# Second block: both heads of a pair transposed in one run of TensorE, the second into an idle weight-tile bank

## The chip, the cores and the metric

One core of one Trainium2 chip runs the whole program in one launch. The metric is the device time of that launch in microseconds (us).

## What is computed

Two transformer blocks follow each other on 256 tokens of width 2048, in fp32. The first (depth 1) mixes a gated MLP, dilated attention and sparse attention, then cross-attends and runs an MLP. The second has two layers; the change lies in their attention. Each layer projects the normed input to queries, keys and values of three branches with heads of 64 columns, attends, norms each branch, projects back, and runs a squared-relu MLP of width 8192:

```python
for l in range(DEPTH_2):
    h = rmsnorm(x, norm_mix[l])
    proj = jnp.einsum('bsd,de->bse', h, w_in[l])
    ...
    oa = window_attention(qa, ka, va, a_sink[l], t5_table)       # A: 8 heads
    ob = neighborhood_attention(qb, kb, vb, b_rpb[l])            # B: 8 heads
    oc = axial_global_attention(qc, kc, vc, c_q_gain[l], c_k_gain[l])   # C: 16 heads
    mix = jnp.concatenate([rmsnorm(oa, ...), rmsnorm(ob, ...), rmsnorm(oc, ...)], axis=-1)
    x = x + mix @ w_o[l]
    x = x + jnp.square(relu(rmsnorm(x) @ w_up[l])) @ w_down[l]
```

Each attention head is a softmax of scores (256 by 256) times values. The kernel computes scores and probabilities with the queries on partitions, but the product with the values needs the keys there, so each head's probabilities are transposed on TensorE between the two.

## The kernel before

**The stream of units.** Almost all time goes into products with weights. A weight tile of 128 by 1024 arrives by DMA (`wt`), ScalarE rounds it to fp32r (`wh`, step "split"), VectorE forms the rest (`wl`), and TensorE multiplies by both. A unit is two such tiles. In an ordinary unit (`unit`, L371) the result of 16 pairs of matmuls lies in one PSUM bank. In a value unit (`value_unit`, L433) the tokens are on partitions: two banks are open at once and held over several units. An ordinary unit's bank is emptied at the start of the next one: ScalarE takes one half out (`tA`, counted by `a_half`), VectorE adds the other (`tB`, counted by `v_sum`).

**The banks.** PSUM has eight banks, in one tensor `ps`. Banks 0 to 2 are the main banks, which the units take in turn (`next_bank`, L295). Banks 3 and 4 (`bS`) hold the scores of the two heads of a pair, bank 5 (`bP`) takes transposes, bank 6 (`bO`) the attention outputs, bank 7 (`bM`) small sums and norms.

**The planner.** `make_plan` (L142) runs in Python before anything is emitted and writes one list of steps; every engine then emits its instructions in the order of that list, so every engine's queue is fixed. Units are the main line. Attention work is written as generators in a list `tasks`. In every unit, at matmul pair 8 (`n in stages`, in `marks`, L322), `step_bg` (L240) moves each generator on by one step. The instructions of all these steps stand together on TensorE between two halves of a unit; below, this is called a run. Functions in the list `at13` are called at pair 13 of the same unit.

**A pair of heads** (`two_heads`, L1193) goes through: scores of both heads into banks 3 and 4, and the exponentials ("score2"); the division, which leaves the probabilities in a tile `sS` (counted by `v_prob`); the transposes; and the product with the values ("av"), one run later. A head's turn (`turn_head`, L1143; `prob_turn`, L2076) is four transposes of 128 by 128 from `sS` into one bank, then one copy of that bank to a tile `sP`: ScalarE copies the first head (L2393, `a_pcopy`), VectorE the second (L2742, `v_pcopy`). The product of the first head with the values waits for `a_pcopy`, that of the second for `v_pcopy`. The first head is turned in the run at pair 8, the second is put on the list `late` and so is turned at pair 13:

```python
        pts = [sP.grab() for _ in hds]
        turn_head(hds[0], pts[0], 0)
        late.append(lambda: turn_head(hds[1], pts[1], 1))
        yield
```

In branch C, and in the last pairs of B, both heads use bank 5, so the second turn waits for the first head's copy (`a_pcopy`). In A and the first pairs of B the second head uses bank 7 (`apart`).

**Waits.** `give` writes down which semaphore counts make a buffer free, `take` hands them to its next user, and `let_go` (L1708) emits them as waits. There are 16 pairs of heads in each of the two layers (C0 to C7, A0 to A3, B0 to B3), so 32 second turns.

Of the kernel before, what the change touches and what calls it, by code (L numbers as in the profile page):

```python
# [141 lines left out]
def make_plan():  # L142

    p = Plan()
# [90 lines left out]
    deferred, pending, at3, at10, at13, after_unit = [], [], [], [], [], []  # L235
    held = {"evac": False, "s1": 0}

    late = []

    def step_bg():  # L240
        held["s1"] = 0
        for g in list(tasks):
            if next(g[0], "end") == "end":
                tasks.remove(g)
                g[1]["done"] = True
        at13.extend(late)
        late.clear()

# [30 lines left out]
    def run_at13():  # L279
        while at13:  # L280
            at13.pop(0)()
# [8 lines left out]
        else:  # L290
            step("mm", h, k, k + 1)

    banks = {"n": 0, "held": set()}

    def next_bank():  # L295

# [49 lines left out]

    def unit_end():
        run_at13()
        while after_unit:
            after_unit.pop(0)()  # L350

# [19 lines left out]
    def unit(parts, nk, src, thin=False, stages=(8,), ahead=2, early=False, tail=False):  # L371

        u = unit_begin(ahead)
        n = 0
        for j, (first, last, ev) in enumerate(parts):
            if first:
                next_bank()
            g = len(groups) - 1
            for k in range(nk):
                marks(n, None if len(parts) == 1 else max(1, 4 - n // 4) if thin else 0, stages, early)  # L380
                if (thin or tail) and n == 11:
                    run_pending()
                h = where[2 * u + n // 8][1]
                end = last and k == nk - 1
                if thin:
                    half = 2 * k // nk
                    tiles[h].append((g, src(j, k % (nk // 2)), k % (nk // 2) == 0, end, half, (k + 1) % (nk // 2) == 0))
                else:
                    tiles[h].append((g, src(j, k), first and k == 0, end, None, end))
                matmuls(h, n % 8)  # L390
                if n % 8 == 7:
                    done[g] = tick("t_used", h)
                    give(("wh", h % 4), done[g])
                elif end:
                    done[g] = tick("t_thin", g)
                n += 1
            if last:
                pending.append((ev, g))
                if j < len(parts) - 1:
                    kept = pending.pop()  # L400
                    run_pending()
                    pending.append(kept)
# [30 lines left out]
    def value_unit(name, ev, stages=(8,), ahead=2, early=False):  # L433
# [3 lines left out]
        if name not in open_values:  # L437
            gs = next_bank(), next_bank()
            banks["held"] |= {p.bank[g] for g in gs}
            open_values[name] = [*gs, 0]  # L440
        g0, g1, k = open_values[name]
        n = 0
        for c in range(2):
            h = where[2 * u + c][1]
# [695 lines left out]

    sS_of, qden, branch_norms = {}, {}, set()

    def turn_head(hd, pt, j):  # L1143
        s = sS_of[hd]
        apart = j == 1 and hd[1] in "AB" and (hd[0], "C") not in branch_norms
        bank = "bM" if apart else "bP"
        step("turn", hd, s, pt, j, apart)
        take(bank, bank, *hd)
        take(("Pt", pt), "Pt", *hd)
        give(("S", s), tick("t_turn", *hd))  # L1150
        sS.held.discard(s)
        give(bank, tick("v_pcopy" if j else "a_pcopy", *hd))

    def av_heads(pr, parts):
        step("av", pr, tuple(parts))
# [37 lines left out]
    def two_heads(pr, qk, v, bias=False, sink=False):  # L1193
# [52 lines left out]
            yield  # L1246
        pts = [sP.grab() for _ in hds]
        turn_head(hds[0], pts[0], 0)
        late.append(lambda: turn_head(hds[1], pts[1], 1))
        yield  # L1250
        while not has("a_v", *v):
            yield
# [303 lines left out]
def program(nc, I, out):  # L1556
    p, feed, tiles, done = make_plan()
    at, free = p.at, p.free
    with ExitStack() as ctx:
# [261 lines left out]
        def _(eng):  # L1821
# [251 lines left out]
                    t = mm(bS[b][:, qt * T:(qt + 1) * T], q[b0:b0 + n, qt * P:(qt + 1) * P], k[b0:b0 + n, 0:T], True, True)  # L2073
                t.then_inc(S.t_score)

            def prob_turn(hd, s, pt, odd, apart):  # L2076
                w.wait_ge(S.v_prob, at["v_prob", *hd])
                bank = bM if apart else bP
                let_go(w, "bM" if apart else "bP", *hd)
                for kt in range(2):  # L2080
                    for qt in range(2):
                        t = turn(bank[:, kt * T + qt * P:kt * T + (qt + 1) * P], sS[s][:, qt, kt * P:(kt + 1) * P])
# [346 lines left out]
        def _(eng):  # L2429
# [183 lines left out]
            for kind, *key in p.steps:  # L2613
# [126 lines left out]
                elif kind == "prob":  # L2740
                    prob(*key)
                elif kind == "turn" and key[3]:  # L2742
                    hd, s, pt, _, apart = key
                    bank = bM if apart else bP
                    w.wait_ge(S.t_turn, at["t_turn", *hd])
                    let_go(w, "Pt", *hd)
                    eng.tensor_copy(sP[pt][:, :, :], bank[:, 0:512].rearrange("p (a b) -> p a b", a=2)).then_inc(S.v_pcopy)
# [339 lines left out]
```

## Time and profile before

| What | us |
| --- | --- |
| median of 3 runs | 3297.06 |
| lowest and highest of them | 3294.58, 3297.74 |
| the profiled execution, its own time | 3295.73 |
| its span, first to last instruction | 3293.9 |
| PE (TensorE) busy | 3266.9 (99%) |
| DVE (VectorE) busy | 2170.3 (66%) |
| ACT (ScalarE) busy | 1621.6 (49%) |
| POOL (GpSimd) busy | 912.7 (28%) |

PE is TensorE's matmuls, and PEld its weight loads, which overlap them. Times in the profile are in us from the start of the span. The attention of the second block's first layer lies between about 1260 and 1470, that of its second layer between about 2300 and 2505. Matmuls are pipelined and their ends are modelled, so the cost of one is read from the distance between starts. Line L1825 is every matmul, whatever it multiplies, and L1828 every transpose, so they are told apart by their tiles: `ps<-x,wh`, `ps<-x,wl` (ordinary units), `ps<-wh,x`, `ps<-wl,x` (value units), `ps<-idt,sS` (a turn, x4), `ps<-sP,vc` or `ps<-sP,va` (product with the values, x8 for a pair).

### The profile page before, as it was taken

Reading aid. Unit: us, or ns where it says so; the run is one execution under the profiler, and the core shown is the slowest. Engines: PE = TensorE matmul, PEld = TensorE weight load, DVE = VectorE, ACT = ScalarE, POOL = GpSimd, SP = SyncE. Lnnn points to the kernel's source line nnn. Section 1 sums busy time; section 2 is a strip of 40 time slices with the busy share of each in tenths; the row PEclk is TensorE's granted clock in tenths of the full one; section 3 lists DMA queues with packets and bytes.
Section 4 is the critical chain, followed back from the end, with each engine's and each line's share of the span. In section 5 each row is a group of like instructions: output and inputs, shape, how many; then the busy total and the mean of one; then the engine's idle time right before and its main releaser. Section 6 shows DMA issues by size and latency. Waiting matters only on the chain.

```text
span 3293.9 us, 48400 instructions
## 1 busy us (share of the span) xinstructions
PE 3266.9 (99%) x19112; PEld 2859.3 (87%) x19112; DVE 2170.3 (66%) x3068; ACT 1621.6 (49%) x2692; POOL 912.7 (28%) x815
## 2 busy tenths in 40 slices
PE   8999999999999999999999999999999999999998
PEld 7989888888888897788888888889788888888887
DVE  6668677654676668778764477555778775457654
ACT  4557464444444545555443344444655544344443
POOL 2434132210232224254320033112336331013221
PEclk9999999999999999999999999999999999999999
DMA  7544546755566554555655556555355566555554
GB/s 258 189 166 148 175 158 210 234 192 188 190 189 194 186 187 134 159 169 184 191 189 195 185 189 190 193 190 179 123 175 170 187 191 194 190 187 190 188 195 143
DMA packets 188280, 604.57 MB, mean 184 GB/s; under 512 B 36597, under 2 KB 41573, under 8 KB 188054
## 3 DMA queue, kind: packets, MB, share of 16 engines
q1 hardware_dynamic: 188054, 601.47, 56.7%
q8 instruction: 152, 2.49, 0.3%
q14 instruction: 74, 0.61, 0.1%
HBM read 599.16 MB, written 8.00 MB: 184 GB/s over the span
## 4 chain that ended last, share of the span: by engine, by line
PE 91%; DVE 5%; ACT 3%; issue 1%; POOL 1%; DMA 0%; DVEq 0%; POOLq 0%; ACTq 0%; SPq 0%
PE ps L1825 90%; DVE wl L2433 2%; ACT sS L2267 1%; ACT wh L2171 1%; PE ps L1828 1%; DVE sS L2437 1%; POOL acc L2792 0%; DVE x L2441 0%; DVE xr L2433 0%; DVE den L2577 0%; ACT tA L2171 0%; DMA wt<-in_w_in 0%; DVE ua L2441 0%; POOL qc L2792 0%; ACT tG L2424 0%
## 5 line engine op out<-in xcount | busy, mean ns | idle before, releaser
L2433 DVE TENSOR_TENSOR wl<-wt,wh 128x1024 fp32r<-128x1024 f32 (+2 forms) x1104 | 1466.4, 1360 | 312.7 <-ACT wh L2171 296.4
L1825 PE MATMUL ps<-x,wh 128*128 128x512 f32 x4448 | 1563.4, 394 | 11.9 <-DVE x L2441 9.5
L1825 PE MATMUL ps<-x,wl 128*128 128x256 f32 x4448 | 1255.2, 282 | 0.0
L2171 ACT ACTIVATE wh<-wt 128x1024 fp32r<-128x1024 f32 (+2 forms) x1104 | 1117.4, 1051 | 275.2 <-PE ps L1825 236.2
L1825 PEld LDWEIGHTS ps<-x,wh 128*128 128x128 f32 x4448 | 837.0, 188 | 192.8 <-DVE wl L2433 13.9
L1825 PEld LDWEIGHTS ps<-x,wl 128*128 128x128 f32 x4448 | 842.6, 189 | 0.6
L1825 PE MATMUL ps<-ua,wh 128*128 128x512 f32 (+1 forms) x2432 | 832.0, 386 | 0.0
L1825 PE MATMUL ps<-ua,wl 128*128 128x256 f32 x2368 | 667.4, 282 | 0.0
L2433 DVE TENSOR_TENSOR tB<-ps,tA 128x256 f32<-128x256 f32 x422 | 177.1, 423 | 724.3 <-ACT tA L2171 724.2
L2171 ACT ACTIVATE tA<-ps 128x256 f32<-128x256 f32 x422 | 159.6, 382 | 945.0 <-PE ps L1825 944.8
L1825 PE MATMUL ps<-ub,wh 128*128 128x512 f32 x1536 | 536.6, 390 | 0.0
L1825 PEld LDWEIGHTS ps<-ua,wh 128*128 128x128 f32 x2432 | 452.3, 188 | 92.7 <-issue 1.4
L2792 POOL TENSOR_TENSOR tB<-tB 128x256 f32<-128x256 f32 x192 | 317.1, 1652 | 739.8 <-DVE tB L2441 739.8
L1825 PEld LDWEIGHTS ps<-ua,wl 128*128 128x128 f32 x2368 | 447.5, 189 | 0.2
L1825 PE MATMUL ps<-ub,wl 128*128 128x256 f32 x1536 | 433.1, 282 | 0.0
L2792 POOL TENSOR_TENSOR xr<-xr,tB 128x256 f32<-128x256 f32 x143 | 119.5, 838 | 859.0 <-DVE tB L2433 856.4
L1825 PEld LDWEIGHTS ps<-ub,wh 128*128 128x128 f32 x1536 | 288.4, 188 | 60.4
L1825 PEld LDWEIGHTS ps<-ub,wl 128*128 128x128 f32 x1536 | 290.3, 189 | 0.0
L2792 POOL TENSOR_TENSOR acc<-acc,tS 128x256 f32<-128x256 f32 x116 | 146.9, 1266 | 103.4 <-ACT tS L2176 94.9
L1825 PE MATMUL ps<-wh,x 128*128 128x512 f32 (+3 forms) x512 | 145.5, 358 | 0.5 <-DVE wl L2433 0.5
L1825 PEld LDWEIGHTS ps<-wh,x 128*128 128x128 f32 x512 | 91.8, 188 | 13.7 <-issue 1.7
L1825 PE MATMUL ps<-wl,x 128*128 128x512 f32 (+3 forms) x256 | 90.4, 353 | 0.0
(233 smaller groups left out, 1855.7 us busy)
## 6 DMA issues: line engine op xcount, KB each, us to landing
wt<-in_w_up SPq DMA_DIRECT2D x384, 512.0 KB, 4.4
wt<-in_w_down SPq DMA_DIRECT2D x384, 512.0 KB, 4.8
wt<-in_w_in SPq DMA_DIRECT2D x156, 512.0 KB, 4.7
wt<-in_w_o SPq DMA_DIRECT2D x64, 512.0 KB, 4.5
wt<-in_w_out SPq DMA_DIRECT2D x32, 512.0 KB, 4.2
wt<-in_w_vb SPq DMA_DIRECT2D x16, 512.0 KB, 4.2
wt<-in_w_va SPq DMA_DIRECT2D x16, 384.0 KB, 3.7
wt<-in_w_vsl SPq DMA_DIRECT2D x8, 512.0 KB, 6.1
```

The source lines that it names most:

```text
L1825: return eng.matmul(o, l, r, start=start, stop=stop, skip_group_check=True)
L1828: return eng.transpose(o, i, idt[0:n, 0:n])
L2171: return eng.activation(o, i, ACT.Copy, **kw)
L2267: eng.activation(sS[s][:, qt, :], bS[b][:, qt * T:(qt + 1) * T], ACT.Exp, bias=nm[:, qt:qt + 1], scale=scale, accum_out=dn[:, qt:qt + 1]). ...
L2433: return eng.tensor_tensor(o, a, b, op)
L2437: return eng.tensor_scalar(o, a, s1, None, op0)
L2792: return eng.tensor_tensor(o, a, b, op)
```

## The change

The second turn is no longer put on `late` but on a new list `turns`, which `step_bg` empties right after it has moved the generators on: in the same unit, at the end of the run at pair 8. There `second_turn` asks `idle_bank` for one of the three main banks that is neither open in the current unit nor waiting to be emptied; the one that is used again last is tried first. If there is one, the turn goes into it and becomes one more user of that bank: it waits for the bank's last reader, and the bank's next unit waits for `v_pcopy`. If there is none, or if emptying is held back, the turn goes to `late` as before, into bank 5 or 7. VectorE still makes the copy.

```diff
--- before.py
+++ after.py
@@ -235,7 +235,7 @@
     deferred, pending, at3, at10, at13, after_unit = [], [], [], [], [], []
     held = {"evac": False, "s1": 0}
 
-    late = []
+    late, turns = [], []
 
     def step_bg():
         held["s1"] = 0
@@ -243,6 +243,7 @@
             if next(g[0], "end") == "end":
                 tasks.remove(g)
                 g[1]["done"] = True
+        run_all(turns)
         at13.extend(late)
         late.clear()
 
@@ -290,7 +291,17 @@
         else:
             step("mm", h, k, k + 1)
 
-    banks = {"n": 0, "held": set()}
+    banks = {"n": 0, "held": set(), "open": None}
+
+    def idle_bank():
+
+        if held["evac"] or banks["open"] is None:
+            return None
+        busy = set(banks["open"])
+        for _, g in pending:
+            busy |= {p.bank[i] for i in (g if isinstance(g, tuple) else (g,))}
+        left = [(banks["n"] + j) % 3 for j in (1, 0, 2) if (banks["n"] + j) % 3 not in busy]
+        return left[0] if left else None
 
     def next_bank():
 
@@ -346,6 +357,7 @@
 
     def unit_end():
         run_at13()
+        banks["open"] = None
         while after_unit:
             after_unit.pop(0)()
 
@@ -376,6 +388,7 @@
             if first:
                 next_bank()
             g = len(groups) - 1
+            banks["open"] = (p.bank[g],) if len(parts) == 1 else None
             for k in range(nk):
                 marks(n, None if len(parts) == 1 else max(1, 4 - n // 4) if thin else 0, stages, early)
                 if (thin or tail) and n == 11:
@@ -439,6 +452,7 @@
             banks["held"] |= {p.bank[g] for g in gs}
             open_values[name] = [*gs, 0]
         g0, g1, k = open_values[name]
+        banks["open"] = (p.bank[g0], p.bank[g1])
         n = 0
         for c in range(2):
             h = where[2 * u + c][1]
@@ -1140,16 +1154,22 @@
 
     sS_of, qden, branch_norms = {}, {}, set()
 
-    def turn_head(hd, pt, j):
+    def turn_head(hd, pt, j, b=5):
         s = sS_of[hd]
-        apart = j == 1 and hd[1] in "AB" and (hd[0], "C") not in branch_norms
-        bank = "bM" if apart else "bP"
-        step("turn", hd, s, pt, j, apart)
-        take(bank, bank, *hd)
+        bank = {5: "bP", 7: "bM"}.get(b, ("main", b))
+        step("turn", hd, s, pt, j, b)
+        take(bank, "turn", *hd)
         take(("Pt", pt), "Pt", *hd)
         give(("S", s), tick("t_turn", *hd))
         sS.held.discard(s)
         give(bank, tick("v_pcopy" if j else "a_pcopy", *hd))
+
+    def second_turn(hd, pt):
+        b = idle_bank()
+        if b is not None:
+            turn_head(hd, pt, 1, b)
+        else:
+            late.append(lambda: turn_head(hd, pt, 1, 7 if hd[1] in "AB" and (hd[0], "C") not in branch_norms else 5))
 
     def av_heads(pr, parts):
         step("av", pr, tuple(parts))
@@ -1246,7 +1266,7 @@
             yield
         pts = [sP.grab() for _ in hds]
         turn_head(hds[0], pts[0], 0)
-        late.append(lambda: turn_head(hds[1], pts[1], 1))
+        turns.append(lambda: second_turn(hds[1], pts[1]))
         yield
         while not has("a_v", *v):
             yield
@@ -2073,10 +2093,10 @@
                     t = mm(bS[b][:, qt * T:(qt + 1) * T], q[b0:b0 + n, qt * P:(qt + 1) * P], k[b0:b0 + n, 0:T], True, True)
                 t.then_inc(S.t_score)
 
-            def prob_turn(hd, s, pt, odd, apart):
+            def prob_turn(hd, s, pt, odd, b):
                 w.wait_ge(S.v_prob, at["v_prob", *hd])
-                bank = bM if apart else bP
-                let_go(w, "bM" if apart else "bP", *hd)
+                bank = ps[:, b, :]
+                let_go(w, "turn", *hd)
                 for kt in range(2):
                     for qt in range(2):
                         t = turn(bank[:, kt * T + qt * P:kt * T + (qt + 1) * P], sS[s][:, qt, kt * P:(kt + 1) * P])
@@ -2740,8 +2760,8 @@
                 elif kind == "prob":
                     prob(*key)
                 elif kind == "turn" and key[3]:
-                    hd, s, pt, _, apart = key
-                    bank = bM if apart else bP
+                    hd, s, pt, _, b = key
+                    bank = ps[:, b, :]
                     w.wait_ge(S.t_turn, at["t_turn", *hd])
                     let_go(w, "Pt", *hd)
                     eng.tensor_copy(sP[pt][:, :, :], bank[:, 0:512].rearrange("p (a b) -> p a b", a=2)).then_inc(S.v_pcopy)
```

Of the 32 second turns, 28 go into a main bank. The second turns of B2 and B3, in both layers, stay where they were.

What moves on TensorE, at pair C1 of the first layer. This is the end of the run at pair 8, before (`kc`, `qc`: scores of a later pair; `c,tG`: a sum for the rotation of queries):

```order
L1825 MATMUL ps<-kc,qc 128x256 [waits a_exp]
L1825 MATMUL ps<-kc,qc 128x256
L1825 MATMUL ps<-c,tG 128x2 [waits v_rope,a_rsq]
L1825 MATMUL ps<-c,tG 128x2
L1825 MATMUL ps<-x,wh 128x512 [waits v_lo]
L1825 MATMUL ps<-x,wl 128x256
L1825 MATMUL ps<-x,wh 128x512
L1825 MATMUL ps<-x,wl 128x256
```

And now:

```order
L1845 MATMUL ps<-kc,qc 128x256 [waits a_exp]
L1845 MATMUL ps<-kc,qc 128x256
L1845 MATMUL ps<-c,tG 128x2 [waits v_rope,a_rsq]
L1845 MATMUL ps<-c,tG 128x2
L1848 MATMUL ps<-idt,sS 128x128 [waits v_sum,v_prob]
L1848 MATMUL ps<-idt,sS 128x128 x3
L1845 MATMUL ps<-x,wh 128x512 [waits v_lo]
L1845 MATMUL ps<-x,wl 128x256
```

The second turn (the last two rows but two) stands between the run's last small matmul and the unit; it waits for `v_sum` of the main bank that it takes, no longer for `a_pcopy`.

Further on, on TensorE, are the rest of that unit and the start of the first value unit behind it. Before:

```order
L1828 MATMUL ps<-idt,sS 128x128 [waits a_pcopy,v_prob]
L1828 MATMUL ps<-idt,sS 128x128 x3
L1825 MATMUL ps<-x,wh 128x512
L1825 MATMUL ps<-x,wl 128x256
L1825 MATMUL ps<-x,wh 128x512
L1825 MATMUL ps<-x,wl 128x256
L1825 MATMUL ps<-x,wh 128x512
L1825 MATMUL ps<-x,wl 128x256
L1825 MATMUL ps<-wh,x 128x512 [waits v_sum,v_lo]
L1825 MATMUL ps<-wl,x 128x512
L1825 MATMUL ps<-wh,x 128x512
L1825 MATMUL ps<-wh,x 128x512 [waits v_sum]
```

And now:

```order
L1845 MATMUL ps<-x,wh 128x512
L1845 MATMUL ps<-x,wl 128x256
L1845 MATMUL ps<-x,wh 128x512
L1845 MATMUL ps<-x,wl 128x256
L1845 MATMUL ps<-wh,x 128x512 [waits v_lo]
L1845 MATMUL ps<-wl,x 128x512
L1845 MATMUL ps<-wh,x 128x512
L1845 MATMUL ps<-wh,x 128x512 [waits v_pcopy]
```

The turn at pair 13 is gone, and the fourth matmul of the value unit, the first into its second bank, waits for `v_pcopy` where it waited for `v_sum`: it is the bank into which C1's second head was turned.

VectorE, around the copy that this `v_pcopy` counts, in the changed kernel (the rows before are the same but for the line numbers, which are lower by 20):

```order
L2597 TENSOR_REDUCE den<-ps 128x2 [waits t_score]
L2453 TENSOR_TENSOR den<-den 128x2 [waits v_max]
L2622 STREAM_SHUFFLE tG<-qc 128x256 [waits t_rsum,a_rgain]
L2453 TENSOR_TENSOR tG<-tG,c 128x256 [waits v_swap]
L2458 TENSOR_SCALAR den<-ps 128x4
L2767 COPY sP<-ps 128x512 [waits t_av,t_turn]
L2453 TENSOR_TENSOR tB<-ps,tA 128x256 [waits g_proj,a_half]
```

The copy (`sP<-ps`) keeps its place behind the maxima of a later pair and the rotation.

It keeps its place for all 28 turns that move. For the four that do not, something else changes: `late` also carries the steps "bsplit" of a branch that has been normed, and a second turn is now put on it only after all generators have moved, so behind them. VectorE at pair B2's copy, before (`ua<-qa,ua` is the low part of a normed tile of branch A):

```order
L2481 COPY rB<-ps 128x256 [waits t_spread]
L2441 SCALAR_TENSOR_TENSOR qa<-qa,par,rB 128x256 [waits a_kept,v_norm]
L2441 SCALAR_TENSOR_TENSOR qa<-qa,par,rB 128x256 [waits a_kept]
L2747 COPY sP<-ps 128x512 [waits t_av,t_turn]
L2433 TENSOR_TENSOR ua<-qa,ua 128x256 [waits a_uhi] x2
L2433 TENSOR_TENSOR tB<-ps,tA 128x256 [waits g_res,a_half] x2
L2433 TENSOR_TENSOR wl<-wt,wh 128x1024 [waits a_hi] x2
```

And now:

```order
L2501 COPY rB<-ps 128x256 [waits t_spread]
L2461 SCALAR_TENSOR_TENSOR qa<-qa,par,rB 128x256 [waits a_kept,v_norm]
L2461 SCALAR_TENSOR_TENSOR qa<-qa,par,rB 128x256 [waits a_kept]
L2453 TENSOR_TENSOR ua<-qa,ua 128x256 [waits a_uhi] x2
L2767 COPY sP<-ps 128x512 [waits t_av,t_turn]
L2453 TENSOR_TENSOR tB<-ps,tA 128x256 [waits g_res,a_half] x2
L2453 TENSOR_TENSOR wl<-wt,wh 128x1024 [waits a_hi] x2
```

In both layers the copies of B2 and B3 stand behind two `ua` steps, each of which waits for ScalarE's high part (`a_uhi`), instead of ahead of them. On TensorE these four turns stay at pair 13. ScalarE's, GpSimd's and the DMA queue's orders stay as they are.

## Rows read from the trace of the kernel before

**Rows 1.** Waits of PE, whole span: line, what for, us in total, times, longest
```profile
PE ps L1825 <- DVE sP L2747: 0.9, 2, 0.5
PE ps L1828 <- ACT sP L2171: 0.7, 2, 0.4
```

**Rows 2.** The chain of waits, 1270 to 1350: start, length, engine, line
```profile
1300.74 3.27 DVE wl L2433 x2
```

**Rows 3.** Timeline of PE, 1347 to 1349: start, length, operation, xcount
```profile
1347.71 0.28 PE L1825 MATMUL ps<-x,wl 128*128 128x256 f32 x1
1347.83 0.60 PE L1828 MATMUL ps<-idt,sS 128*128 128x128 f32 x4
1348.18 0.48 PE L1825 MATMUL ps<-x,wh 128*128 128x512 f32 x1
1348.50 0.28 PE L1825 MATMUL ps<-x,wl 128*128 128x256 f32 x1
```

**Rows 4.** Timeline of PE, 1295 to 1300
```profile
1295.52 0.63 PE L1825 MATMUL ps<-wh,x 128*128 128x512 f32 x2
1295.99 0.40 PE L1825 MATMUL ps<-wl,x 128*128 128x512 f32 x1
...
1297.95 1.82 PE L1825 MATMUL ps<-sP,vc 128*64 128x256 f32 x8
```

**Rows 5.** Timeline of DVE, 1297 to 1335 (idle time before a row would stand in brackets)
```profile
1297.95 0.68 DVE L2747 COPY sP<-ps 128x512 f32<-128x512 f32 x1
...
1334.25 0.69 DVE L2747 COPY sP<-ps 128x512 f32<-128x512 f32 x1
```

**Rows 6.** Timeline of PE, 1308 to 1346
```profile
1308.03 2.13 PE L1825 MATMUL ps<-sP,vc 128*64 128x256 f32 x8
...
1318.42 1.30 PE L1825 MATMUL ps<-sP,vc 128*64 128x256 f32 x8
...
1333.58 0.39 PE L1825 MATMUL ps<-x,wh 128*128 128x512 f32 x1
...
1344.57 1.09 PE L1825 MATMUL ps<-sP,vc 128*64 128x256 f32 x8
```

**Rows 7.** Timeline of ACT, 1301 to 1302
```profile
1301.56 0.37 ACT L2176 ACTIVATE tS<-ps 128x256 f32<-128x256 f32 x1
```

**Rows 8.** Timeline of PE, 2370 to 2371 (second layer)
```profile
2370.12 0.39 PE L1825 MATMUL ps<-x,wh 128*128 128x512 f32 x1
```

**Rows 9.** Timeline of DVE, 2370 to 2372 (second layer)
```profile
2370.84 0.69 DVE L2747 COPY sP<-ps 128x512 f32<-128x512 f32 x1
```

**Rows 10.** Timeline of PE, 1382 to 1459
```profile
1382.24 0.48 PE L1825 MATMUL ps<-x,wh 128*128 128x512 f32 x1
...
1412.30 0.50 PE L1825 MATMUL ps<-x,wh 128*128 128x512 f32 x1
...
1418.51 2.05 PE L1825 MATMUL ps<-sP,va 128*64 128x256 f32 x8
...
1457.57 1.33 PE L1825 MATMUL ps<-sP,vb 128*64 128x256 f32 x8
```

**Rows 11.** Timeline of DVE, 1382 to 1458 (idle before it and its end in brackets)
```profile
1382.02 0.42 DVE L2433 TENSOR_TENSOR tB<-ps,tA 128x256 f32<-128x256 f32 x1 [1.25 <-ACT tA L2171]
...
1412.54 0.42 DVE L2433 TENSOR_TENSOR tB<-ps,tA 128x256 f32<-128x256 f32 x1 [1.38 <-ACT tA L2171]
...
1457.09 0.68 DVE L2747 COPY sP<-ps 128x512 f32<-128x512 f32 x1
1457.69 0.75 DVE L2433 TENSOR_TENSOR ua<-qa,ua 128x256 fp32r<-128x256 f32 x2
```

**Rows 12.** Busy time in windows: stretch, length, busy of each engine, granted clock, DMA
```profile
490.00:495.00 5.00, 3.45 (x18) 2.49 (x16) 5.00 (x7) 3.37 (x8) 3.60 (x3) 0.97 0.57 190
495.00:500.00 5.00, 4.43 (x17) 3.76 (x16) 4.32 (x7) 2.32 (x3) 1.36 (x3) 0.50 0.63 199
500.00:505.00 5.00, 5.00 (x27) 4.38 (x27) 0.99 (x3) 0.71 (x3) 0.10 (x1) 0.85 0.48 175
```

## The prediction

> **What bounds the kernel now.** I read who TensorE waited for, the chain of waits, and then the timelines of PE, DVE and ACT around the turns. Matmuls fill the span, so only what lengthens or shortens TensorE's own stream counts. Of all its waits, the copies of turned heads end 0.9 us (VectorE's) and 0.7 us (ScalarE's) [rows 1]. A second thing to see: from about 1270 to 1338 the chain of waits doesn't run through TensorE at all. It alternates between ScalarE and VectorE, and the low parts of two weight tiles, 3.27 us, are its largest piece [rows 2]. There VectorE works behind TensorE. The copy of C1's second head starts at 1297.95, though its unit, transposes included, was over before 1295.5 [rows 4]. No idle time stands before it, so it waits in VectorE's queue and not for the turn [rows 5].
>
> **The break that goes.** At pair 13, four transposes stand between wide matmuls. The last `wl` starts at 1347.71, the next `wh` at 1348.18, and it takes 0.32 to its `wl` at 1348.50 [rows 3]. Without a break these distances would be 0.12 (the transposes start 0.12 after the `wl`) and 0.23 (two 512-column matmuls in 0.47 us, 1295.52 to 1295.99 [rows 4]). The break costs 0.35 + 0.09 = 0.44 us. In a run the transposes remain: three steps of (0.60 - 0.27) / 3 = 0.11 and a fourth, 0.43 to 0.44 us. So a moved turn saves about 0.01, and 28 of them 0.3 us, 0.15 in each layer. The change removes a place and next to no work. It saves waits for `a_pcopy` too: the two of 0.35 us [rows 1] are C6's, one in each layer, since C6's second turn no longer needs bank 5.
>
> By the Trainium skill, "TensorE: Matmul & The Clock Gate", section "Back-to-back issue gap", matmuls of 128 columns with their weight loads are sustained at some 81 ns each. Four transposes would by that be 0.32 us in a run, the saving 0.12 each and 3.4 us in all. The trace doesn't agree: theirs are 0.11 us apart.
>
> **The waits that come: VectorE's copy now holds a main bank.** The order shows where. The fourth matmul of the first value unit waits for C1's copy. Today it is the second of the two that start at 1295.52, and starts one step of 0.235 ahead of the `wl` at 1295.99, at 1295.75 [rows 4]. The copy ends at 1297.95 + 0.68 = 1298.63 [rows 5], and nothing that VectorE does before it depends on the moved turn. That is a stall of 2.9 us. But part of it comes back. The product of a pair with the values takes 1.09 us when both copies are there, and 1.82, 2.13 and 1.30 us for C1, C2 and C3, because the second copy is late [rows 4, 6]. A TensorE that comes later meets finished copies: 0.73 + 1.04 + 0.21 = 1.98 us back, and 0.9 left. Next, C5's second turn takes the bank that the unit at 1333.58 needs [rows 6], and its copy ends at 1334.25 + 0.69 = 1334.94 [rows 5]. So that unit starts 1.36 us later than before, whatever was left of the first stall. Minus C6's 0.35, branch C costs 1.0 us. In the second layer the same unit starts at 2370.12 [rows 8] and its copy ends at 2371.53 [rows 9]: 1.41 - 0.35 = 1.06.
>
> **Waits for the bank's last reader.** A1's turn must stand by 1382.24, the bank's `tB` is done at 1382.02 + 0.42 = 1382.44: 0.2, with the signal's way 0.25 us. A3's would be 0.7 us (1412.54 + 0.42 against 1412.30) [rows 10, 11]. But the product behind it takes 2.05 us, 0.96 over 1.09, for want of its copy [rows 10], so I count it as absorbed.
>
> **The copies that swap places.** B2's turn doesn't move, but its copy now stands behind two `ua` steps of together 0.75 us [rows 11]. They wait for ScalarE's high part besides, so the copy ends 0.7 to 1.0 us later than 1457.77. The product with the values starts at 1457.57 and already waits for it (1.33 against 1.09 us [rows 6, 10]), so all of that lies on the path. I take 0.9 us, in both layers. The ends are 0.7 and 1.0; it would be nothing only if the product waited for something else as long. B3's turn is the same edit and counted at nothing: its copy is covered by the unit half that follows, and if that cover failed it would cost as much as B2's.
>
> **The sum.** First layer 1.0 + 0.25 + 0.9 - 0.15 = 2.0, second 2.06: **4.1 us**.
>
> **The unknown: TensorE's clock.** It was granted at 2.4 GHz (1.00) in the whole attention. After a stretch in which TensorE was busy 3.45 of 5 us it fell to 1.2 GHz (0.50), and stayed there for the next 5 us and part of another 5, in all 5 + 0.75 / 0.5 + 0.15 / 0.5 = 6.8 us [rows 12]. A stall of 2.9 us is a larger hole than that, but a full stream stands on both sides. The price of one fall lies between nothing and 3.4 us less what the later wait gives back (0.4), 3.0. I take one fall in the two stalls, and half the length, since the array is full again at once: 1.7, less the 0.4 or somewhat more, 1.0. A fall in neither and in both lie equally far from it. Total **5.1 us**.
>
> The profiled execution took 3295.73, 1.3 below the median of the three runs; on it the sum gives 3300.8, on the median **3302.2 us**.
>
> **The rivals.** A difference of 0.2%, 6.6 us, is about what a measurement of this kernel can tell from none.
>
> (a) Nothing is given back. It holds if ScalarE and VectorE are themselves held by TensorE, so that the copies move back as it does. Against it: ScalarE takes C1's product at 1301.56 [rows 7], though that ended about 1299.8 (1297.95 + 1.82), so there are 1.8 us of room; TensorE will be 2.9 - 0.7 = 2.2 us late there. It decides beyond 1.8, so a small part is likely. Price: 2.9 + 1.36 + 0.25 + 0.7 + 0.9 - 0.35 - 0.15 = 5.6 in a layer, 11.2 in all: 3308.3, slower.
>
> (b) The clock falls twice and for as long as in rows 12: 4.1 + 2 x 3.0 = 10.1, 3307.2, slower.
>
> (c) The stalls don't come, because VectorE's copy comes up to 2 us earlier with its earlier turn. Then the waits of rows 1 go, 1.6 us, and 0.3 from the breaks, against 1.8 for the swapped copies: -0.1, 3297.0. Against it stands the copy without idle time before it [rows 5]; only where VectorE did wait for a turn would this help.
>
> (d) Transposes behind others in a run cost only what their columns cost in a wide matmul. A `wl` of 256 columns gives way after 0.12 us [rows 3], so 128 columns would be 0.06 and four 0.24, against 0.44 for the break: 0.20 x 28 = 5.6 us less, so 5.1 - 5.6 = -0.5, 3296.6. Against it: 0.11 us between the transposes of one turn [rows 3]. The Trainium skill's 81 ns, from the section named above, would give 5.1 - 3.4 = 1.7, 3298.8, by the same mechanism. With (c) it gives -5.7, and with short waits that rows 1 don't list it could pass -6.6: faster.
>
> That the turns don't move is excluded by the order: 28 of 32 do.
>
> **How the numbers follow.** Forecast 0.61, of which 0.13 lies above 6.6 us (two falls, with a little of (a)): 0.48 no change, 0.13 slower. (a) 0.08 and (b) 0.06, both slower. (c) 0.17 and (d) 0.05, both no change. (c) with (d) 0.03, faster. Together 0.03 faster, 0.70 no change, 0.27 slower. The range reaches down to (c) without its last part, 3296.8, and up to (b), 3307: outside are (a), a part of (b), some of (c) and (d), and (c) with (d). No case of both signs competes; the forecast's own range is 3301.2 (no fall) to 3303.2 (two short ones).
>
> **What would show it.** Right: PE idle 2.9 us before a `ps<-wh,x` near 1296 and again near 2332, ended by DVE `sP` L2767; 0.4 to 1.4 us near 1334 and 2370; PE's waits for DVE `sP` 6 to 9 us in all; products of C1 to C3 at 1.1 to 1.3 us; a granted clock below 1.00 near 1300 or 2336; B2's product over 2 us. Eight transposes in a row 0.11 us apart. Wrong: no wait at 1296, or a C3 product still over 2 us with TensorE late, or transposes below 0.1 us apart. The forecast fails if VectorE's lag is not what holds the copy.

## The result, and the profile after

The changed kernel took 3300.91 us (median of 16 runs, 3296.35 to 3306.08), the kernel before 3294.98 (16 runs, 3292.83 to 3297.74). The ratio is 1.0016, with a 95% interval of 1.0009 to 1.0023: 5.9 us slower, a small loss that is clear of the noise, and less than the 0.2% (6.6 us) up to which the forecast speaks of no change. The profiled execution took 3298.90, against 3295.73 before: 3.2 us slower. So about half of the 5.9 lies in the one trace; on the rest the experiments throw some light. Of the runs below, one of e10 (4961.71 us, mean clock 0.605) and one of e11 (8306.62 us, 0.469) were slow ones: the medians listed include them, the ratios and the counts of clocks do not.

The waits of PE over the whole span (line, what for, us in total, times, longest). The changed kernel's lines are 20 higher than those of the kernel before:

```profile
PE ps L1845 <- DVE sP L2767: 6.8, 6, 2.8
PE ps L1845 <- POOL den L2812: 3.0, 3, 1.0
...
PE ps L1848 <- DVE tB L2453: 1.1, 2, 0.6
```

The first answers to the 0.9 us of [rows 1] and is what was forecast. ScalarE's 0.7 us for `sP` of [rows 1] is gone. The last is the wait for the bank's last reader, forecast too. The second was not: the kernel before has one such wait, of 1.0.

The timeline of PE at the first stall (start, length, operation, xcount, idle before and what ended it), where [rows 4] had no idle time:

```profile
1295.57 0.40 PE L1845 MATMUL ps<-wh,x 128*128 128x512 f32 x1
1298.77 0.50 PE L1845 MATMUL ps<-wh,x 128*128 128x512 f32 x1 [2.81 <-DVE sP L2767]
...
1301.06 1.09 PE L1845 MATMUL ps<-sP,vc 128*64 128x256 f32 x8
...
1310.37 1.09 PE L1845 MATMUL ps<-sP,vc 128*64 128x256 f32 x8
...
1319.69 1.09 PE L1845 MATMUL ps<-sP,vc 128*64 128x256 f32 x8
```

The stall is there, and the products with the values of C1, C2 and C3 take 1.09 us each where they took 1.82, 2.13 and 1.30 [rows 4, 6]. What they lost to late copies before is what they give back now.

The timeline of DVE shows the copy where it was:

```profile
1297.96 0.15 DVE L2458 TENSOR_SCALAR den<-ps 128x4 f32<-128x4 f32 x1
1298.03 0.68 DVE L2767 COPY sP<-ps 128x512 f32<-128x512 f32 x1
```

It starts 0.08 us later than in [rows 5], though its transposes start 1.7 us earlier (at 1291.85 instead of 1293.58), and again with no idle time before it.

C5's unit starts at 1334.85 instead of 1333.58 [rows 6]:

```profile
1334.85 0.47 PE L1845 MATMUL ps<-x,wh 128*128 128x512 f32 x1 [0.18 <-DVE sP L2767]
```

And eight transposes of one run, both heads of a pair:

```profile
1338.82 1.09 PE L1848 MATMUL ps<-idt,sS 128*128 128x128 f32 x8
```

That is (1.09 - 0.27) / 7 = 0.117 us for each step, the same as in the break of [rows 3] or a little more. The move saves no time on the array.

**The wait that nobody forecast.** At 1443 TensorE waits for a tiny operation of GpSimd:

```profile
1443.01 0.49 PE L1845 MATMUL ps<-idt,den 128*128 128x128 f32 x2 [1.04 <-POOL den L2812]
```

GpSimd there, in the kernel before (timeline of POOL):

```profile
1435.51 2.53 POOL L2792 TENSOR_TENSOR sS<-sS,c 128x256 f32<-128x256 f32 x4 [2.74 <-DMA sS<-rpm]
1437.99 0.74 POOL L2792 TENSOR_TENSOR kb<-tB,rT 128x256 f32<-128x256 f32 x1
1438.69 0.73 POOL L2792 TENSOR_TENSOR accs<-accs,tS 128x256 f32<-128x256 f32 x1
1439.40 0.71 POOL L2792 TENSOR_TENSOR den<-den,mhalf 128x2 f32<-128x2 f32 x1
```

and in the changed kernel:

```profile
1438.67 1.23 POOL L2812 TENSOR_TENSOR sS<-sS,c 128x256 f32<-128x256 f32 x2 [1.18 <-DMA sS<-rpm]
1439.86 0.74 POOL L2812 TENSOR_TENSOR kb<-tB,rT 128x256 f32<-128x256 f32 x1
1440.56 0.75 POOL L2812 TENSOR_TENSOR accs<-accs,tS 128x256 f32<-128x256 f32 x1
1441.26 1.70 POOL L2812 TENSOR_TENSOR den<-den,mhalf 128x2 f32<-128x2 f32 x1
```

The last of B3's bias transfers (`sS<-rpm`) landed 4.06 us after its issue instead of 2.67, GpSimd waited 1.18 for it, and `den` took 1.70 instead of 0.71. VectorE's part of it, before and after (timeline of DVE, from one kernel each):

```profile
1440.40 2.36 DVE L2433 TENSOR_TENSOR wl<-wt,wh 128x1024 fp32r<-128x1024 f32 x2 [1.08 <-ACT wh L2171]
```

```profile
1441.04 2.48 DVE L2453 TENSOR_TENSOR wl<-wt,wh 128x1024 fp32r<-128x1024 f32 x2 [1.08 <-ACT wh L2191]
```

Before, `den` had begun 1.0 us ahead of the pair of `wl`; now it comes 0.2 us behind it, and ends 1.0 us late. The second layer shows the same (1.71 us). TensorE's delay against the kernel before goes from 0.65 to 1.95 us across this place in the first layer, from 2.23 to 3.43 in the second. It is the largest single term of the 3.2 us. Whether the change is what makes the transfer land late is taken up below, and stays open.

### The profile page after: what moved, and what is told of

It reads as the page before. It is cut to its first block, busy times and chain, and to the rows that moved or that the text cites. A ratio compares the mean times of both kernels' runs of the same rounds, so it can differ in the third digit from the quotient of the medians.

```text
span 3297.1 us, 48398 instructions
## 1 busy us (share of the span) xinstructions
PE 3261.6 (99%) x19112; PEld 2856.3 (87%) x19112; DVE 2171.6 (66%) x3068; ACT 1622.7 (49%) x2692; POOL 913.0 (28%) x815
## 4 chain that ended last, share of the span: by engine, by line
PE 90%; DVE 5%; ACT 2%; POOL 1%; issue 1%; DMA 0%; SPq 0%; DVEq 0%; POOLq 0%; ACTq 0%
PE ps L1845 89%; DVE wl L2453 2%; PE ps L1848 1%; ACT wh L2191 1%; DVE sS L2457 0%; POOL acc L2812 0%; DVE x L2461 0%; ACT sS L2287 0%; DVE xr L2453 0%; DVE den L2597 0%; DMA sS<-rpm 0%; ACT sS L2276 0%; ACT tA L2191 0%; DMA wt<-in_w_in 0%; POOL sS L2812 0%
```

## The experiments

Each is an edit of the changed kernel, with 11 runs (5 of e4 and of e9). e1, e6, e3 and e4 ran on one chip, the others on another, each group beside 27 or 21 runs of the kernel before, with medians of 3295.46, 3295.49 and 3294.99; the ratios are against those. "Delay" is the start of the same wide matmul of TensorE against the kernel before, in the profiled executions. At 1260, where the programs have not yet differed, it already lies between -1.14 (e2) and 1.78 (e9), so what counts is how it changes across a place, and a difference of 1 us between two profiled totals says little by itself.

| kernel | what moves | profiled | median | ratio, 95% |
|---|---|---|---|---|
| changed | 28 turns | 3298.90 | 3300.91 | 1.0009 to 1.0023 |
| e1 | all but C1 and C5 | 3296.00 | 3299.16 | 1.0001 to 1.0019 |
| e6 | the bank, not the place | 3296.87 | 3299.44 | 1.0004 to 1.0022 |
| e3 | A and B | 3298.51 | 3298.64 | 1.0001 to 1.0019 |
| e4 | 28, the copies ahead too | 3307.21 | 3307.79 | 1.0024 to 1.0049 |
| e9 | 28, two copies on ScalarE | 3308.33 | 3308.33 | 1.0028 to 1.0053 |
| e2 | C1 | 3299.36 | 3299.07 | 1.0001 to 1.0019 |
| e5 | 28, B2 and B3 listed as before | 3297.61 | 3299.60 | 1.0006 to 1.0023 |
| e7 | all but C1, C5; B2, B3 as before | 3294.05 | 3295.50 | 0.9993 to 1.0011 |
| e10 | C without C1 and C5 | 3295.05 | 3293.93 | 0.9987 to 1.0005 |
| e11 | A | 3296.89 | 3295.32 | 0.9990 to 1.0009 |

In e1, e6, e3, e9 and e2 the copies of B2 and B3 stand behind the two `ua` steps, as in the changed kernel; in e4, e5, e7, e10 and e11 they stand as before.

### Is it C1's and C5's bank? (e1)

```
     def second_turn(hd, pt):
-        b = idle_bank()
+        b = None if hd[1:3] in (("C", 1), ("C", 5)) else idle_bank()
```

> The second turns of C1 and C5 go back to the 13th pair and to bank 5; the other 24 stay in the run. Theory (VectorE's copy holds a main bank while one of VectorE's wide subtractions is ahead of it): the 2.9 us stall at 1296 and 2332 and the 1.3 us at 1334 and 2370 are gone; of them 1.98 were given back at the next products, so the net is 1.0 + 0.35 per layer less C6's share: 1.5 to 2.5 us in all, 3298.5 to 3299.5 where the changed kernel stands at 3300.9, and the two waits of PE for L2767 gone. Rival (what was lost is the wait for GpSimd's den, 1.2 us per layer at 1441 and 2478): the time stays within 0.5 us of the changed kernel and that wait stays 1.0 long. Rival (a stall makes the granted clock fall in some executions): the runs' mean clock is higher than the changed kernel's and their spread narrower.

The waits of PE in e1:

```profile
PE ps L1845 <- POOL den L2812: 2.0, 2, 1.0
...
PE ps L1845 <- DVE sP L2767: 1.1, 2, 0.7
```

The stall at 1296 and its twin in the second layer are gone, and branch C gains where it lost: from 1294 to 1350 the delay goes from -0.79 to -1.39 (changed kernel: 0.04 to 0.81). The profiled execution is 2.9 us under the changed kernel's. Branch C gives 1.4 of it in the first layer and 0.9 in the second (delay -0.32 to -0.94). But 0.9 was there before the attention began: the clock fall of [rows 12] was shorter in e1's execution (granted clock 0.70 and 0.96 in 495:500 and 500:505, against 0.53 and 0.79 in the changed kernel's). The wait for `den`, the first rival, is there in the first layer and gone in the second. The median is only 1.8 lower, inside what was expected, but not clear of the noise of the two medians. Not one of 11 runs had a mean clock under 0.997, against 5 of 16 of the changed kernel. What holds e1's other runs above its profiled one is not in this trace; e7, below, says more.

### Bank or place? (e6)

```
         if b is not None:
-            turn_head(hd, pt, 1, b)
+            late.append(lambda: turn_head(hd, pt, 1, b))
```

> All 28 second turns are at the 13th pair again, but into the main bank that was idle when the step bodies ran: the bank without the place. Theory (what costs is that a main bank waits for VectorE's copy, wherever the turn stands): C1's copy is then behind the same wide subtraction and ends no earlier, so the stall of about 2.9 us stays, and with a break of 0.44 per pair again the time is within 1 us of the changed kernel's. Rival (what costs is the place, by the order of VectorE's list): the stalls are gone and the time is that of the kernel before, 3295 to 3296.

```profile
1298.49 0.50 PE L1845 MATMUL ps<-wh,x 128*128 128x512 f32 x1 [2.76 <-DVE sP L2767]
```

The stall is there in full (timeline of PE) though the turn stands where it always stood. Branch C costs 0.90 in the first layer (delay -0.19 to 0.71), against the changed kernel's 0.77, and 0.37 in the second, against 0.23. So the bank is what costs in branch C, and the place of the turn gives next to nothing. The median lies 1.5 us under the changed kernel's, a little outside the 1 us that was expected; `den` was late in neither layer of e6 (0.71 and 0.72 us).

### Branches A and B alone (e3)

```
-        b = idle_bank()
+        b = idle_bank() if hd[1] in "AB" else None
```

> Only the second turns of the A and B pairs (12) are moved; branch C's 16 stay as before. Theory (banks of branch C): nothing of the stalls at 1296, 1334, 2332 and 2370 is left; what remains is A1's 0.25, A3's 0.7 absorbed and B2's swapped copy, 0 to 1 us per layer: 3295 to 3297. Rival (GpSimd's den waits for a bias transfer and belongs to B2 and B3's part of the change): the wait of 1.0 at 1441 and 2478 is still there, and the time is 2.4 us over the kernel before, 3297.4.

Branch C shows no difference (delay 0.25 to 0.26). The rival's wait is there in the first layer: `den` 1.75 us long at 1440.7, delay 0.22 to 1.42. In the second layer `den` takes 0.71, and another loss shows, 0.9 us at the value product of B2 (timeline of PE, 2493 to 2498):

```profile
2495.50 2.24 PE L1845 MATMUL ps<-sP,vb 128*64 128x256 f32 x8
```

It takes 1.36 us in the layer where `den` was late. In all six kernels with the swapped copies (12 layers) one of the two losses shows and never both: 0.7 net at B2 where `den` was in time, none where it was late. A TensorE held up by 1.2 us at 1441 comes late enough to find B2's swapped copy done. The profiled execution lies above both theories' figures, 3298.51, though.

### The copy moved forward with the turn (e4)

```
-        turns.append(lambda: second_turn(hds[1], pts[1]))
+        second_turn(hds[1], pts[1])
```

> The second turn directly behind the first, ahead of the run's other steps, and its copy ahead of the wide subtractions of the run in VectorE's list. Theory (the bank is held because the copy stands behind a subtraction of 2.0 us): the copy ends some 2 us earlier, C1's stall of 2.9 and C5's of 1.3 go or shrink to a few tenths, but PE meets the wait for v_sum that the other steps covered: 2.9 at C0, 0.5 at A0, 1.8 at A3 per layer, given back in part at later units. The time is 3296 to 3303. Rival (the copy's place doesn't matter, the place of the turn does): as the changed kernel, 3300 to 3301, with the wait for L2767 still 6.8 in sum.

The copy, on DVE's timeline, and PE's waits:

```profile
1293.05 0.47 DVE L2461 SCALAR_TENSOR_TENSOR ua<-ps,par,ua 128x256 fp32r<-128x256 f32 x1
1293.45 0.68 DVE L2767 COPY sP<-ps 128x512 f32<-128x512 f32 x1
```

```profile
PE ps L1848 <- DVE tB L2453: 9.8, 11, 2.9
...
PE ps L1845 <- POOL kb L2812: 6.4, 2, 3.4
```

The copy ends 4.6 us earlier and C1's stall is gone, as the theory has it. The turns now wait for `tB` eleven times, 9.8 us in all, about what the theory's list comes to for two layers (10.4). But the scores of a pair of B wait for GpSimd's `kb` in each layer, 6.4 us in all, which neither theory named, and the granted clock fell twice (below). 3307.8 is outside what was expected. An early copy is to be had only with a turn that waits.

### The copy on another engine (e9)

```
-        give(bank, tick("v_pcopy" if j else "a_pcopy", *hd))
+        give(bank, tick("v_pcopy" if j and hd[1:3] not in (("C", 1), ("C", 5)) else "a_pcopy", *hd))
...
-                elif kind == "turn" and not key[3]:
+                elif kind == "turn" and (not key[3] or key[0][1:3] in (("C", 1), ("C", 5))):
```

> The changed kernel, with the second copies of C1 and C5 alone on ScalarE instead of VectorE; the turns keep their place and their main bank. Theory (the stall comes from the copy's place in VectorE's list, not from the bank or from the place of the turn): ScalarE is idle from 1292.8 to 1296.4 there, so the copy ends near 1293.5 and the stalls at 1296, 1334, 2332 and 2370 are gone; the profiled execution is that of the kernel without C1 and C5 moved, 3295.5 to 3297, plus or minus GpSimd's 1.2 per layer. Rival (a third main bank in use by a turn is what makes PE wait, whoever empties it): the 2.9 at 1296 and 2332 stay, and the time is the changed kernel's.

Wrong on both sides. ScalarE's timeline, and TensorE's:

```profile
1298.10 0.56 ACT L2288 ACTIVATE sS<-ps,den 128x256 f32<-128x256 f32 x1 [3.69 <-DVE den L2454]
...
1300.73 0.51 ACT L2192 ACTIVATE qc<-qc,par 128x256 f32<-128x256 f32 x1
1301.15 0.58 ACT L2192 ACTIVATE sP<-ps 128x512 f32<-128x512 f32 x1
```

```profile
1301.78 0.50 PE L1845 MATMUL ps<-wh,x 128*128 128x512 f32 x1 [4.15 <-ACT sP L2192]
```

I had read ScalarE's idle stretch as room for the copy. But the copy is issued in its place in the program, which on ScalarE is behind the exponentials of the next pair, and they wait for VectorE's maxima. The stall grew to 4.15 us. This bears out from the other side that the copy's place in its engine's list sets the stall; it doesn't bear out that VectorE is the wrong engine for it.

### One stall alone, and the clock (e2)

```
-        b = idle_bank()
+        b = idle_bank() if hd[1:3] == ("C", 1) else None
```

> Only C1's second turn is moved (2 of 28), with B2 and B3's turns issued in the changed order. Theory: C1's stall of 2.9 stays, 2.0 of it given back by C3, so 0.9 to 1.0 per layer of it is left, and 0.7 to 0.9 per layer at the value products at 1457 or 1.2 at 1441: 3.2 to 4.2 over the kernel before, 3298 to 3299.5 in the profiled execution. If a stall makes TensorE's clock fall in some executions, some of these runs have a mean clock of 0.996 or less, as 5 of 16 of the changed kernel and 3 of 11 of the kernel with the bank alone had and none of 27 of the kernel before. Rival (falls come by chance or from other stretches): no run at 0.996 or less.

The same stall in both layers, 2.98 us each. In the first, the delay goes from -1.20 to -0.62: a net 0.58. In the second it goes from 0.04 to 2.82, a net 2.78. The windows of the second layer show what happened there (stretch, PE, PEld, DVE, ACT, POOL busy, granted clock, DMA share, GB/s):

```profile
2331.00:2334.00 3.00, 1.03 (x5) 0.51 (x4) 2.83 (x9) 1.50 (x5) 0.00 (x0) 1.00 0.65 228
2334.00:2337.00 3.00, 2.16 (x5) 1.78 (x6) 1.31 (x5) 2.97 (x9) 2.65 (x4) 0.50 0.00 0
2337.00:2340.00 3.00, 3.00 (x11) 1.70 (x12) 2.62 (x2) 0.81 (x1) 0.40 (x1) 0.50 0.14 22
2340.00:2343.00 3.00, 3.00 (x22) 1.71 (x19) 1.14 (x5) 1.24 (x3) 0.73 (x1) 0.86 0.80 303
```

```profile
2334.84 0.80 PE L1845 MATMUL ps<-wh,x 128*128 128x512 f32 x1 [2.81 <-DVE sP L2767]
```

The clock falls to 1.2 GHz inside the stall and stays there 6.8 us, where the kernel before had no fall in the attention. Without a fall the second layer costs some 0.5 less than the first (changed kernel 0.77 and 0.23, e6 0.90 and 0.37), so the long fall cost 2.78 - 0.58 + 0.5 = 2.7 us. e5's execution has a short one, 3.4 us from 2335.0, at the same stall: branch C's net there is 1.74 us (0.30 to 2.04), against the 0.23 of the changed kernel in the same layer without a fall, so 1.5. In e4 and e9 the clock fell at or behind stalls too (at 1279.3 and 1429.5, at 1302.2 and 2343.3). Over all runs: of the kernels with C1's stall (changed, e6, e2, e5, e9) 20 of 54 had a mean clock of 0.996 or less; of those without it (e1, e3, e7, e10, e11) 3 of 53, and of the 75 runs of the kernel before beside the experiments none (e4, with other stalls, had 2 of 5). Only the profiled executions show where a fall was; for the other runs the mean clock shows that one more or a longer one was there, not its place. C6's second turn stands as before in e2, and its wait is gone all the same (delay -0.10 to -0.62 at C6): a TensorE that comes later finds the first head's copy done. The rest of e2's time is B2's swapped copies, 0.7 in each layer.

### The list of B2 and B3 as before (e5)

```
-        turns.append(lambda: second_turn(hds[1], pts[1]))
+        if pr[1] == "B" and pr[2] > 1:
+            late.append(lambda: turn_head(hds[1], pts[1], 1, 5))
+        else:
+            turns.append(lambda: second_turn(hds[1], pts[1]))
```

> The changed kernel, but the second turns of B2 and B3 put on the list of the 13th pair where the kernel before puts them, so that their copies stand in VectorE's list as before. Theory (B2's copy behind two other operations, and GpSimd's den behind VectorE's subtraction, are one part of the change, and the first hides the second): the eight value products at 1457 to 1461 take 1.35, not 2.2, and without GpSimd's wait the time falls by 1.2 per layer to 3296.5 to 3297 in the profiled execution. Rival (the den wait hangs on how late the last bias transfer lands, which the order does not set): the wait of 1.0 at 1441 or 2478 stays in at least one layer, at 3297.5 to 3299.

The value products lose nothing (delay 0.32 ahead of B2's, 0.31 behind), so the 0.9 us belong to the swapped copy. But the rival was right on `den`: 0.71 us in the first layer and 1.70 in the second, the bias transfer 3.31 and 4.02 us. The second wait does not come from the order of the copies. My theory that both are one part of the change fell.

### Towards a better version (e7, e10, e11)

e7 is e1 and e5 together. In e10 and e11 the turns that stay go straight on the list of pair 13:

```
-        turns.append(lambda: second_turn(hds[1], pts[1]))
+        if pr[1] == "C" and pr[2] not in (1, 5):
+            turns.append(lambda: second_turn(hds[1], pts[1]))
+        else:
+            late.append(lambda: turn_head(hds[1], pts[1], 1, 7 if pr[1] in "AB" and (pr[0], "C") not in branch_norms else 5))
```

and in e11 the condition is `pr[1] == "A"`.

> C1, C5, B2 and B3 as before, the other 20 turns in the run: the best that the parts promise. Theory: no stall for L2767 over 1, no late value products, and C6's 0.35 and part of the break saved in each layer: 0 to 1.5 under the kernel before, 3294 to 3296, interval across 1. Rival (den wait from the transfer): as before plus 1.2 to 2.4, 3296.5 to 3298.

> Only the second turns of branch C but C1 and C5 are moved (12 of 28); A and B stand as in the kernel before. Theory: C6's 0.35 per layer and a little of the break are saved, nothing is lost, and GpSimd's den meets no late transfer as long as branch A's turns stand where they were: 0.7 to 1.5 under the kernel before, 3294 to 3295, den 0.71 long in both layers. Rival (the late transfer is chance, whatever is moved): den 1.7 long in at least one layer, 3295 to 3296.5.

> Only the second turns of branch A are moved (8 of 28). Theory: A1's and A3's waits for v_sum come and are covered again, C and B as before: 3295.5 to 3297. If moving A's turns is what makes the last bias transfer of B3 land late (3.3 to 4.1 us after its issue in ten of twelve cases with A's turns moved, 2.4 to 3.0 without), then GpSimd's den is 1.7 long in one or both layers and the time is 1.2 to 2.4 more; if not, the transfer takes 2.4 to 3.0.

e7 has the median of the kernel before (3295.50 and 3295.49), inside what was expected. It also prices two parts of the change over many runs, which no single trace can. e5 and e7 ran side by side and differ only in C1 and C5: their medians lie 4.1 us apart (95% interval, by resampling the runs: 2.0 to 7.4), their profiled executions 3.6. e1 and e7 differ only in where the copies of B2 and B3 are listed: 3.7 apart (0.9 to 5.9), 2.0 in the profiled executions; but these two ran on different chips, so a part may be the chip's. With C1's and C5's stalls there (the changed kernel against e5), the same edit of the list is worth 1.3, which is within the noise.

`den` in the first and the second layer of e7, then of e10:

```profile
1439.45 0.72 POOL L2815 TENSOR_TENSOR den<-den,mhalf 128x2 f32<-128x2 f32 x1
...
2475.54 1.73 POOL L2815 TENSOR_TENSOR den<-den,mhalf 128x2 f32<-128x2 f32 x1
```

```profile
1439.25 0.70 POOL L2815 TENSOR_TENSOR den<-den,mhalf 128x2 f32<-128x2 f32 x1
...
2474.92 0.71 POOL L2815 TENSOR_TENSOR den<-den,mhalf 128x2 f32<-128x2 f32 x1
```

e10 gains in branch C (delay 0.61 to -0.02 from 1294 to 1350, -0.21 to -0.89 in the second layer) and loses nothing behind it. Its median is 1.1 us under the kernel before, and the interval includes 1: none of the versions is shown to be faster. e11 has the late transfer in its second layer (4.0 us, `den` 1.68) and not in its first (3.10). Over the profiled executions, with branch A's turns moved the last transfer took 3.1 to 4.1 us (fourteen cases, `den` late in seven of them: changed 2, e1, e3, e5, e7, e11 1 each, e9 none). With A's turns left as before it took 2.4 to 3.0 in the six of before, e2 and e10, and `den` was never late. e6, with A's turns in their place but in another bank, lies between (3.5 and 3.8 us, `den` 0.71 and 0.72). e4, where all stands otherwise, is not counted. One thing is clear-cut in all 22 cases: `den` was late in the seven in which the transfer took 3.90 us or more, and in none in which it took 3.84 or less. Why a transfer that nothing in the order moves should land later is not settled, and with it whether the change causes the loss or the executions only differ in it.

## Why the prediction was right, and where it was not

The forecast of 3302.2 us stood 1.3 above the median of 16 runs. That is two errors that partly cancel: it stood on a kernel before of 3297.06 (three runs), where 16 runs give 3294.98, and it took 5.1 us for the change, where 5.9 were measured. It was right in class and near in size. The nearness is luck in part: the 1.8 for B2's copies didn't show in the profiled execution, the 2.5 for `den` were not in the sum, and the clock was priced too low.

- **VectorE's queue holds the bank: right.** Forecast 2.9 us, measured 2.98 and 2.96. Given back by the products of C1 to C3: forecast 1.98, measured 3.12 - 0.99 = 2.1 in the first layer. C5: forecast 1.36, measured 1.36 (the delay at 1336). Branch C's net was 0.77 in the first layer, against 1.0; in the second it was 0.23, against 1.06. There TensorE came into the branch 1.89 late, and VectorE's copy at C5 ended only 1.08 later than before (at 2372.61), so the delay after it was 2.72 and not 1.89 + 1.41. A sum made for each layer from zero leaves that out. The stop at C5 was no shorter for it (it adds 0.43 in both layers); what the second layer had more of was time to give back, 2.6 against 2.1, because C2's copy had been later there. Rival (a) is excluded by the products at 1.09 us, rival (c) by the copy at 1298.03. The second half of C2's product in the kernel before, second layer (timeline of PE; the first half starts at 2344.08):

```profile
2345.49 1.08 PE L1825 MATMUL ps<-sP,vc 128*64 128x256 f32 x4 [0.33 <-DVE sP L2747]
```

- **The break: right, small.** A transpose in the run takes 0.117 us. Rival (d) is excluded, and so is the figure of 81 ns of the Trainium skill ("TensorE: Matmul & The Clock Gate", section "Back-to-back issue gap") for these fp32 transposes.
- **C6's wait: somewhat undersized.** The delay falls by 0.5 to 0.6 us at C6, not by 0.35. But e2 gains the same with C6's turn unmoved, so a late TensorE alone brings it, and not only the other bank.
- **A1 and A3: right.** In the first layer 0.16 net by A's middle against 0.25, and nothing left of A3.
- **B2's swapped copy, 0.9 in each layer: the term that failed in the profiled execution.** In the changed kernel B2's product took 1.36 us at 1459.53, and the delay didn't grow. The mechanism is real: e6 paid 0.7 net in both layers, e3 and e1 in the second. But I took the state of TensorE ahead of it as given, and 1.2 us lost at 1441 covered it. Over the runs it may weigh more than in the traces: e1's and e7's medians lie 3.7 apart, against 1.8 forecast for both layers. Why is open.
- **What the sum lacked: GpSimd's `den`,** 1.2 to 1.3 in each layer. The prediction looked at no operation of GpSimd, because its order didn't change. Its work stood only 1.0 us ahead of VectorE's `wl` at 1440, and that distance, not its order, was what mattered.
- **The clock: right in kind, too small in size.** A fall was priced at 1.0: measured 1.5 for a short one (e5) and 2.7 for a long one (e2). The changed kernel's profiled execution had none at the stalls, and stands 3.2 over the kernel before; the medians stand 5.9 apart. That the 2.7 between them are falls in part fits the clocks of the runs (3296.35 to 3298.36 us in the five with a mean clock of 0.998, 3300.66 to 3306.08 in the five at 0.996 or less). e1, without the stall, has a median of 3299.16 and no fall of that size, so falls are not all of it.

Without the clock, 4.1 was forecast, 1.8 of it for B2's copies. Measured were 3.2: 2.5 for `den`, 1.0 for branch C, and some 0.4 less at the value products behind `den`.

## What to carry to other kernels

Before a resource is handed to an engine that lags, look at how long it will hold it: the idle bank was idle for TensorE, but VectorE took it 3 us later, and moving the writer forward does not move the reader. The places of such a reader in its engine's list decide, on whichever engine it is (e4, e9). And add up the terms of a change in order of time: a stall covers the later ones (`den` covered B2's copy) and a small delay can push two engines on to each other that were 1 us apart.

## What was not expected of the hardware

- GpSimd and VectorE exclude each other for whole operations. `den`, of two columns, takes 0.70 to 0.72 us when it starts ahead of VectorE's `wl<-wt,wh`, and 1.68 to 1.75 when it starts behind it; in e3 it was only 0.04 us behind, and took the 1.75. In all seven late cases it ends 0.56 us behind the end of the first `wl`. This is what the Trainium skill states ("SBUF — State Buffer", section "SBUF: two separate sides"): an operation of VectorE with two SBUF inputs and one of GpSimd lock a shared port pair, and the later one blocks for the whole of the first. The traces agree: at this place it is all or nothing, with no case between 0.72 and 1.68. They show it the other way round too: in the kernel before, where a `wl` takes 1.23 us alone, the second of the two below starts at 1547.27, while GpSimd is still at work, and ends at 1548.90, 1.08 us behind GpSimd's end: it takes 1.63. Behind `den` itself, of two columns, little is lost: in e7's first layer a `wl` that started 0.01 us behind it took 1.27. The timelines of DVE and POOL in the kernel before:

```profile
1546.13 2.77 DVE L2433 TENSOR_TENSOR wl<-wt,wh 128x1024 fp32r<-128x1024 f32 x2
```

```profile
1546.29 1.53 POOL L2792 TENSOR_TENSOR tB<-tB 128x256 f32<-128x256 f32 x1 [0.36 <-DVE tB L2441]
```

- The granted clock can fall inside a stall of 2.8 us in an otherwise full stream, and need not: e2's two stalls are alike, and the clock fell only in the second; in the changed kernel's profiled execution it fell in neither.
- A 64 KB transfer, issued 0.66 us behind the one before it and with the same neighbours in the queue, landed after 2.4 to 4.1 us.
